# One diffusion step on one core: the turn stage joined into the hyena stage, its first folds taken tile by tile, and half of the filter's lower parts on VectorE

## The reference

```python
h = _rmsnorm(x, norm1_g) * (1.0 + scale1) + shift1
proj = h @ w_in
q, k, v, u_hy, gates = jnp.split(proj, SPLITS, axis=-1)
...
o_attn = _diff_attention(q_att, k_all, v_all, lam, lam_init, attn_subln_g)
o_hy = _hyena(u_hy, conv_w, conv_b, ...)
g_attn, g_hy = jnp.split(jax.nn.sigmoid(gates), 2, axis=-1)
merged = g_attn * (o_attn @ w_br_attn) + g_hy * (o_hy @ w_br_hy)
x = x + gate1 * (merged @ w_out)
h2 = _rmsnorm(x, norm2_g) * (1.0 + scale2) + shift2
x = x + gate2 * (jnp.square(jax.nn.relu(h2 @ w_up)) @ w_down)
```

```python
def _hyena(u, ...):
    u = _short_conv(u, conv_w, conv_b)
    v, x1, x2 = jnp.split(u, 3, axis=-1)
    hf = _hyena_filters(L, w1, b1, w2, b2, w3, freq)
    z = x1 * _fftconv(v, hf[:, 0], hy_bias[0])
    return x2 * _fftconv(z, hf[:, 1], hy_bias[1])
```

## Time and profile before

| | |
|---|---|
| median of three runs | 2918.12 us (2911.11 to 2922.55) |
| the profiled execution | 2921.78 us |
| its span | 2920.0 us |
| TensorE busy | 2699.8 us, 92% |
| VectorE / ScalarE / GpSimd busy | 43% / 31% / 28% |
| DMA over the span | 329.99 MB, mean 113 GB/s |
| granted TensorE clock, mean | 0.962 |

### The profile page before, as it was taken

How to read it: one execution, slowest core, us unless ns; L and a number is a source line. 1 busy time by engine, 2 the same in 40 slices (tenths; PEclk the granted TensorE clock), 3 DMA queues, 4 the chain that set the end, 5 groups by cost and what they waited for, 6 DMA issues and landing times. The chain is left out here.

```text
span 2920.0 us, 36034 instructions
## 1 busy us (share of the span) xinstructions
PE 2699.8 (92%) x14723; PEld 2312.2 (79%) x14723; DVE 1260.9 (43%) x1874; ACT 901.1 (31%) x1510; POOL 814.5 (28%) x567
## 2 busy tenths in 40 slices
PE   9757999989999999998888799798999999999998
PEld 7546887878888898887667588687888888888886
DVE  6466664445656445443677521226212212212215
ACT  2333221045555454553311331214121121121121
POOL 2565885111000110100233132212232232232330
PEclk9968999999999999999899799899999999999999
DMA  5756775442213321302766533510111111111101
GB/s 182 228 176 234 232 238 192 142 161 98 82 64 104 109 86 60 109 32 80 284 201 229 181 128 125 205 44 30 37 42 38 37 37 37 44 37 37 37 29 73
DMA packets 103938, 329.99 MB, mean 113 GB/s; under 512 B 12497, under 2 KB 30515, under 8 KB 103390
## 3 DMA queue, kind: packets, MB, share of 16 engines
q1 hardware_dynamic: 77038, 233.30, 23.2%
q0 software_dynamic: 26736, 94.38, 9.5%
HBM read 240.61 MB, written 78.64 MB: 109 GB/s over the span
## 5 line engine op out<-in xcount | busy, mean ns | idle before, releaser
L89 PE MATMUL tl_b<-tl_hi,tl_whi 128*128 128x512 f32 (+1 forms) x960 | 344.8, 359 | 20.8 <-DVE tl_lo L2350 15.0
L90 PE MATMUL tl_b<-tl_lo,tl_whi 128*128 128x512 f32 (+1 forms) x960 | 342.4, 357 | 0.0
L91 PE MATMUL tl_b<-tl_hi,tl_wlo 128*128 128x512 f32 (+1 forms) x960 | 341.7, 356 | 0.0
L2291 DVE SCALAR_TENSOR_TENSOR tl_x<-tl_b,all_mod,tl_x 128x512 f32<-128x512 f32 (+1 forms) x216 | 142.5, 661 | 374.6 <-PE tl_b L91 363.0
L2185 POOL TENSOR_TENSOR tl_wlo<-tl_raw,tl_whi 128x1024 fp32r<-128x1024 f32 x72 | 178.2, 2477 | 444.9 <-ACT tl_whi L2104 444.9
L89 PE MATMUL tl_b<-tl_uhi,tl_whi 128*128 128x512 f32 (+1 forms) x768 | 275.2, 358 | 3.5 <-POOL tl_ulo L2195 3.5
L91 PE MATMUL tl_b<-tl_uhi,tl_wlo 128*128 128x512 f32 (+1 forms) x768 | 276.6, 360 | 0.0
L89 PE MATMUL at_out<-h_hi,at_whi 128*128 128x424 f32 (+1 forms) x672 | 264.1, 393 | 12.4 <-POOL at_wlo L496 10.6
L90 PE MATMUL tl_b<-tl_ulo,tl_whi 128*128 128x512 f32 (+1 forms) x768 | 274.5, 357 | 0.0
L681 DVE TENSOR_REDUCE at_nmax<-at_s 128x1 f32<-128x1280 f32 (+1 forms) x160 | 196.8, 1272 | 112.1 <-PE at_s L548 111.4
L496 POOL TENSOR_TENSOR at_wlo<-at_raw,at_whi 128x1024 fp32r<-128x1024 f32 x28 | 66.2, 2363 | 626.7 <-ACT at_whi L597 626.7
(11 more groups left out here) (290 smaller groups left out, 5810.5 us busy)
## 6 DMA issues: line engine op xcount, KB each, us to landing
tl_raw<-in_w_tail SPq DMA_DIRECT2D x72, 512.0 KB, 3.5
hy_tab<-in_hy_tab POOLq DMA_DIRECT2D x68, 512.0 KB, 5.0
hd_wa<-in_w_adaT SPq DMA_DIRECT2D x32, 512.0 KB, 4.4
at_raw<-in_w_proj SPq DMA_DIRECT2D x28, 512.0 KB, 4.7
fd_in<-in_xT SPq DMA_DIRECT2D x16, 640.0 KB, 4.2
s_gatesT<-at_pad SPq DMA_DIRECT2D x16, 640.0 KB, 2.9
mg_gate<-s_gatesT SPq DMA_DIRECT2D x16, 640.0 KB, 5.2
fd_in<-in_w_ada SPq DMA_DIRECT2D x16, 512.0 KB, 3.6
```

The source lines that it names most:

```text
L89: pe.matmul(out, w_hi, x_hi, start=first, stop=False)
L90: pe.matmul(out, w_hi, x_lo, start=False, stop=False)
L91: return pe.matmul(out, w_lo, x_hi, start=False, stop=last)
L2291: dve.scalar_tensor_tensor(out=x1[:, n, at:at + m], in0=bank[x % GEMM_BANKS][:, 0:m], scalar=g.mod[:, gate, SEG_OF[c]:SEG_OF[c] + 1], in1= ...
```

## The change

It has three parts.

1. **v comes earlier.** In attention, at step 71 (the second unit of the last head), SP loads v's four row tiles from convT into the places of the q and k buffers that head 6 has left. Hyena finds them there: its `v` lies at the same addresses, within the space that the spectra's products (`gc`, `gs`) will use later.
2. **Turn is gone; hyena does its work.** TensorE transposes v at hyena's start (`turn_v`), ACT moves z and splits the folds alternately, and DVE folds as tiles come. The first two forward steps run together (TOGETHER = 2), over one time tile after the other, each waited for alone, which needs four table units at once. Forward steps rotate over four bank pairs (FWD_PAIR). The inverse of tile 0 waits for the lower parts frequency tile by frequency tile, and its runs are reordered (PARTS) so that both halves' first four frequency tiles come first and p is whole after the third run; ACT copies it then. x1 isn't stored transposed any more: SP loads its four row tiles, two of them only when DVE has read the last spectrum of order 0, over whose buffers they lie, and TensorE transposes eight blocks behind each inverse tile of order 0 (`turn_x1`); DVE multiplies with them in their bank. The first two spectra of order 1 are loaded only after the last of these. POOL's wait for all lower parts (L1618) and its order are otherwise as before.
3. **Head.** In order 1 DVE makes 11 of the 21 lower parts (ON_DVE: pair 0's five, none of pairs 1 and 2, four of pair 3, two of pair 4), with a semaphore for each pair. The last four squared tiles are no longer added by DVE: TensorE sums each over the partitions, ten columns a tile (`token_sum`), and DVE adds the five sources. The modulations come ahead of the last pairs.

```diff
+                if u == HY_V_AT:
+                    sp.wait_ge(conv_out, 16 * U_U)
+                    for m in range(2):
+                        sp.wait_ge(qk[m], (HEADS - 1) * UNITS)
+                    for c in range(CHT):
+                        sp.dma_start(hy_v[c][:], g.convT[c]).then_inc(hy_v_in, 16)
...
+    LATE_SUMS = list(range(len(SQUARE_AT), KD))
+    SOURCES = 1 + len(LATE_SUMS)
+    ON_DVE = [range(5), (), (), range(4), range(2)]
...
                     for i, x in enumerate(slots(p)):
+                        if o and i in ON_DVE[p]:
+                            continue
                         pool.wait_ge(split_hi, o * SPLITS + SLOTS[p] + i + 1)
                         pool.tensor_tensor(lo_of(x), eo[(o * PAIRS + p) % 2][:, i], hi_of(x), ALU.subtract
-                                           ).then_inc(split_lo, 1)
+                                           ).then_inc(lows[p] if o else split_lo, 1)
...
+            def token_sum(src, x):
+                for tt in range(TT):
+                    mm = pe.matmul(p_sum[:, src, tt:tt + 1], x[:, tt * P:(tt + 1) * P], g.ones[:, 0:1], start=True,
+                                   stop=True)
+                mm.then_inc(token_sums, 1)
+            def late_sum(n):
+                k = LATE_SUMS[n]
+                pe.wait_ge(squared, k + 1)
+                token_sum(n + 1, stream[(X_AT + k) % STREAM])
...
                 if o == 0:
                     for p in range(len(EARLY), PAIRS):
                         taps_of(1, p)
-                    pe.wait_ge(summed, KD)
-                    evacuated(pe, R - 1)
-                    evacuated(pe, R - 2)
-                    evacuated(pe, R - 3)
-                    for tt in range(TT):
-                        mm = pe.matmul(p_sum[:, tt:tt + 1], acc[:, tt * P:(tt + 1) * P], g.ones[:, 0:1], start=True,
-                                       stop=True)
-                    mm.then_inc(token_sums, 1)
+                        if p == len(EARLY):
+                            for x in range(R - NB, R):
+                                evacuated(pe, x)
+                            pe.wait_ge(summed, len(SQUARE_AT))
+                            token_sum(0, acc)
+                        elif p < PAIRS - 1:
+                            late_sum(0)
+                    for n in range(1, len(LATE_SUMS)):
+                        late_sum(n)
...
             def pair(o, p):
                 k = o * PAIRS + p
                 eo_k = eo[k % 2]
-                if k >= 2:
+                if 2 <= k < PAIRS + 2:
                     dve.wait_ge(split_lo, slots_before(k - 1))
+                elif k >= 2:
+                    dve.wait_ge(lows[p - 2], len(slots(p - 2)))
                 dve.wait_ge(taps, 2 * k + 2)
...
+            def lower_slots(p):
+                for i, x in enumerate(slots(p)):
+                    if i in ON_DVE[p]:
+                        dve.wait_ge(split_hi, SPLITS + SLOTS[p] + i + 1)
+                        dve.tensor_tensor(lo_of(x), eo[(PAIRS + p) % 2][:, i], hi_of(x), ALU.subtract
+                                          ).then_inc(lows[p], 1)
...
+                modulations()
+                lower_slots(0)
                 for p in range(len(EARLY), PAIRS):
                     pair(1, p)
-                    sum_up(len(SQUARE_AT) + p - len(EARLY))
-                sum_up(KD - 1)
-                dve.wait_ge(token_sums, 1)
-                dve.tensor_scalar(var[:], p_sum[:], 1.0 / D, EPS, ALU.mult, ALU.add).then_inc(var_done, 1)
+                    lower_slots(p)
+                dve.wait_ge(token_sums, SOURCES)
+                dve.tensor_reduce(tot[:], p_sum.rearrange("p s t -> p t s"), AX.X, ALU.add).then_inc(tot_done, 1)
+                dve.wait_ge(tot_done, 1)
+                dve.tensor_scalar(var[:], tot[:], 1.0 / D, EPS, ALU.mult, ALU.add).then_inc(var_done, 1)
                 dve.wait_ge(std_done, 1)
                 dve.reciprocal(rstd[:], std[:]).then_inc(rstd_done, 1)
...
-def stage_turn(nc, g, z):
...
+PARTS = [(0, 0), (1, 1), (0, 1), (1, 0)]
+FWD_PAIR = [[0, 1, 2, 3, 0, 1, 2, 3, 0, 1], [1, 3, 2, 0, 1, 3, 2, 0, 1, 0]]
+TOGETHER = 2
...
-        spec = [st.sb(f"spec{s}", [P, SPEC, CH]) for s in range(2)]
+        spec_at = st.place()
+        spec = [st.sb(f"spec{s}", [P, SPEC - s, CH]) for s in range(2)]
+        x1 = [st.over(f"x1{c}", spec_at + c * 4 * T, [P, T]) for c in range(2)] + [
+            st.sb(f"x1{c}", [P, T]) for c in range(2, CHT)]
...
         def _(sp):
+            sp.wait_ge(tab_in[2 * TOGETHER - 1], 16)
             sp.dma_start(bias[:], g.d["hy_bias"]).then_inc(bias_in, 16)
+            for c in range(2, CHT):
+                sp.dma_start(x1[c][:], g.convT[CHT + c]).then_inc(x1_in, 16)
+            sp.wait_ge(fwd_read, FTILES)
+            for c in range(2):
+                sp.dma_start(x1[c][:], g.convT[CHT + c]).then_inc(x1_in, 16)
...
+            def turn_v(n):
+                mirror, tile = JOBS[n]
+                if n >= 4:
+                    pe.wait_ge(z_moved, n - 3)
+                for c in range(CHT):
+                    mm = pe.transpose(bank[4 + n % 4][:, c * P:(c + 1) * P], v[c][:, stored_columns(mirror, tile)],
+                                      g.ident[:])
+                mm.then_inc(v_turned, 1)
+            def turn_x1(tile):
+                if tile == 0:
+                    pe.wait_ge(x1_in, 16 * CHT)
+                    pe.wait_ge(fwd_read, FTILES)
+                else:
+                    pe.wait_ge(zdone, tile)
+                for mirror in range(2):
+                    for c in range(CHT):
+                        mm = pe.transpose(bank[mirror][:, c * P:(c + 1) * P], x1[c][:, stored_columns(mirror, tile)],
+                                          g.ident[:])
+                mm.then_inc(x1_turned, 1)
+            def banks_free(o, j):
+                pairs = FWD_PAIR[o]
+                if pairs[j] in pairs[:j]:
+                    last = max(x for x in range(j) if pairs[x] == pairs[j])
+                    pe.wait_ge(fwd_read, o * FTILES + last + 1)
+                elif o == 0 and pairs[j] >= 2:
+                    pe.wait_ge(z_moved, len(JOBS))
+                elif o and pairs[j] == 0:
+                    pe.wait_ge(zdone, HT)
+                elif o and pairs[j] == 1:
+                    pe.wait_ge(fwd_read, FTILES)
+                elif o:
+                    pe.wait_ge(q_read, HT if pairs[j] == 2 else HT - 1)
+            def forward(o, j, c, tiles, last):
...
+                for tile in tiles:
+                    mm = products(pe, forward_banks(o * FTILES + j)[c][:], t_hi[:, at + tile], t_lo[:, at + tile],
+                                  hi[:, tile], lo[:, tile], tile == first, tile == last)
+                if tiles[-1] == last:
+                    mm.then_inc(runs, 1)
+            for n in range(LAT_JOBS):
+                turn_v(n)
             for o in range(2):
...
+                for j in range(TOGETHER):
+                    banks_free(o, j)
+                for tile in range(HALF_T[0]):
+                    pe.wait_ge(fold_lo, o * HT + tile + 1)
+                    for j in range(TOGETHER):
+                        for c in range(2):
+                            forward(o, j, c, [tile], HALF_T[0] - 1)
+                    if o == 0 and tile == 0:
+                        for n in range(LAT_JOBS, len(JOBS)):
+                            turn_v(n)
+                for j in range(TOGETHER, FTILES):
+                    banks_free(o, j)
+                    if j == LAT_FT:
+                        pe.wait_ge(fold_lo, o * HT + HT)
+                    tiles = range(HALF_T[0]) if j < LAT_FT else range(HALF_T[0], HT)
                     for c in range(2):
...
+                        forward(o, j, c, tiles, tiles[-1])
+                for i in range(HT):
+                    n = o * HT + i
+                    if i < 2:
+                        pair = 2 + n % 2
+                        last = max(x for x in range(FTILES) if FWD_PAIR[o][x] == pair)
+                        pe.wait_ge(fwd_read, o * FTILES + last + 1)
+                    else:
+                        pe.wait_ge(q_read, n - 1)
+                    for x, (q, half) in enumerate(PARTS):
+                        hi, lo = (gs_hi, gs_lo) if half else (gc_hi, gc_lo)
+                        odd = half ^ q
+                        if i < HALF_T[0]:
+                            unit, at = FWD_U + 4 * i + x, 0
+                            tiles = range(LAT_FT // 2 * odd, LAT_FT // 2 * (odd + 1))
...
                         for k, tile in enumerate(tiles):
+                            if i == 0 or i == HALF_T[0]:
+                                pe.wait_ge(g_lo, 2 * (o * FTILES + tile + 1))
+                            mm = products(pe, bank[4 + 2 * (n % 2) + q][:], t_hi[:, at + k], t_lo[:, at + k],
+                                          hi[:, tile], lo[:, tile], x < 2 and k == 0,
```

(25 more changed lines are left out.)

188 lines of the change are left out of this document (72 added, 116 removed).

## The result

The changed kernel takes 2893.28 us (median of 4 runs, 2890.10 to 2895.84) against 2919.92 before (median of 4, 2911.11 to 2922.55): 26.6 us less, ratio 0.9916, 95% interval 0.9900 to 0.9931. The forecast was 2894.5. The profiled executions are further apart, 2921.78 and 2890.10 (spans 2920.0 and 2888.3): 31.7 us.

A forecast was written before the change was run, and what follows sets the result against it. TensorE, busy 92% of the span, was taken as the bound, so gains come from shortening its gaps. Hyena -18.3 and head -5.3 sum to -23.6: 2898.2 us profiled, 2894.5 for the median, range 2880 to 2909.

The forecast's parts named there:

- Hyena, predicted -18.3: All of hyena: earlier start, later loads in both orders and an earlier p copy together save 18.3 us.
- Start, -27.4: Start of hyena: with v resident and no turn stage, first product at 1384.7 instead of 1412.15; bounds 24.5 to 29.
- Order 0, +7.3 +2.0 -3.2: Hyena's first order: late loads until inverse tile 1 ends +7.3 us, x1's transposes +2.0, order 1 starting sooner -3.2.
- Order 1, +3.6 -0.6: Hyena's second order: the same late tables cost 3.6 us up to inverse tile 1's end; earlier p copy saves 0.6.
- the two queue orders that the prediction named: POOL's queue in hyena: unit 5's table behind spectrum 2 (4.6 us gap), table 21 behind all lower parts (about 7).
- Rival 1: Hyena's feed is not short, queues run further ahead: 6.6 us off each order, 2881 us; chance 0.24.
- rival 3: Hyena's forward passes: starved feed leaves a gap and half clock each round, +20 us, 2938; chance 0.06.
- Head, predicted -5.3: Head: divided lower parts and sums on TensorE bring order 1's first product to 177.8 from 183.11; bounds 0 and 10.
- the chain is now splits and pairs, not sums: Head, before order 1's first product: last split ends at 170.3, TensorE's token sums already at 168.4.
- Rival 2: The head brings nothing and hyena's late loads take the longest landing, 12.7 us back, 2907; chance 0.17.
- Step 7 of order 0: Hyena's forward pass: this step ends at X+39.9, X being the end of the joined first four runs.
- The bounds of 3, 5 and 4 us: Uncertainty of hyena's start (3), the head (5) and the feed (4), given as 2885 to 2904 around 2894.5.

The follow-up runs named there:

- e3: Changed kernel, but all of v turned and four folds done before hyena's first product; hyena from last attention output to merge 249.28 us, by medians 8.2 slower than the changed kernel.
- e4: Changed kernel, but v loaded after the last head's last output instead of during that head; hyena from last attention output to merge 249.82 us, +7.1.
- e5: Changed kernel, but GpSimd's forward loop issues each table a step earlier and ahead of the spectrum; hyena 13.9 us shorter, 10.6 by the medians.
- e7: Changed kernel, but table 21 and the four tables behind it issued ahead of GpSimd's wait for the last lower parts; hyena 6.4 us shorter, 6.5 by medians.
- e1: Kernel before with only the head's part of the change; 10.7 us less than before, ratio 0.9967 (0.9953 to 0.9980).
- e8: Changed kernel, but x1's first two parts issued at the eighth and ninth product, tenth spectrum in the p copies' place; hyena 242.50 us, -0.2; medians 1.0 apart.
- e11: Changed kernel with the edits of e5, e7 and e8 together; 2861.18 us (2853.36 to 2869.10), ratio to before 0.9813.
- e2: Changed kernel with the old head, so only the turn and hyena's part; 17.9 us less than before, ratio 0.9940 (0.9925 to 0.9955).
- e6: Changed kernel, but table 21 alone issued ahead of GpSimd's wait for the last lower parts; hyena 2.9 us shorter, 3.7 by the medians.

## Why the prediction was right, step by step

**Hyena, predicted -18.3, measured 260.99 to 242.72 = -18.27.** That the sum is exact to a tenth is luck in part; the terms are off by up to 1 us, each way.
- Start, -27.4: measured -27.74. e3 and e4 give two shares of it, 6.6 for going tile by tile and 7.1 for v's early load. The rest is x1's transposes and the chain in front of them.
- Order 0, +7.3 +2.0 -3.2 = +6.1: from first product to first product of order 1 it took 112.56 before and 1488.15-1369.84 = 118.31 after, +5.75. Inside it the joined steps ended at 1382.0, 12.1 us after the first product instead of 14.8, because the first product already ran in 0.50 us; the stall for table 5 was 3.92 instead of 4.6, its slow clock 2.7 instead of 1.5; the last lower part stood 56.8 us behind the joined steps (56.6 predicted), tile 1 began 61.4 behind them (61.3), x1's wait and its transposes before it.
- Order 1, +3.6 -0.6 = +3.0: measured (1601.55-1488.15)-(1634.39-1524.71) = +3.7, with the two stalls where they were expected, 3.96 and 5.82 us.

The mechanism was right as well: e5 and e7 took the two queue orders that the prediction named out of the way, and the stalls went, 13.9 and 6.4 us. Of the signs it named, the first product stands 11.0 us after the last output (10 to 12), the table waits are 3.92 and 3.96 (4 to 5), inverse tile 1 starts 7.15 us after tile 0 in order 0 and 5.82 in order 1 (about 7), and the last transposes of x1 wait 2.31 (2 or less). Rival 1, a feed that isn't short, is refuted by the 15.3 us of table waits; rival 3 by there being one such stall in each forward pass and not six.

**Head, predicted -5.3: right in size, wrong in what ends the chain.** Nine profiles with the changed head (the changed kernel, e1, e3 to e8, e11) have a head stretch of 36.8 us in the mean, 5.1 less than 41.84. But "the chain is now splits and pairs, not sums" fell. Counted from the end of order 0 (141.3 there, 134.8 here), the prediction had the last split end at 29.0, the sums at 27.1 and the first product at 36.5. Measured: VectorE done with the last pair's lower parts at 26.2, the sums at 31.3, the first product at 37.6. Pairs and splits were 2.5 us quicker, the sums 4.2 slower, since the row that I had taken at 2.2 us a sum ran at 1.2 GHz, 4.3 each (granted clock 0.50 from 134.6 to 175.6); VectorE stood 5.09 us for it. The pairs were quicker since VectorE's five lower parts for pair 0 took 5.25 us, not the 8.7 of strict alternation: GpSimd's first part waited for ScalarE's split until 136.57, so three of the five ran alone at 0.68 us, and only the last two took 1.75 each. In the three profiles where the row of three sums took 9.8 us instead of 12.96 (part of it at the full clock) the stretch is 34.3 to 34.5, otherwise 36.5 to 38.7. Rival 2 is refuted: e1 has the head's gain without hyena's change, and the stalls are 3.9 us, not longer.

**Slips in the working.** Step 7 of order 0 comes to X+39.5 and not 39.9 (11.5 and five times 5.6), and inverse tile 1 of order 1 was given 12.8 us where order 0 had 12.3, without a reason. The bounds of 3, 5 and 4 us give 2882.5 to 2906.5 when added up, not 2885 to 2904. The tables' waits before the change are 0.8 us in all, not 1 to 2. Rival 3's limit, a gap of 2.2 us behind which products run at 1.2 GHz, isn't one: the last section has a gap of 2.31 us with either outcome.

**What the prediction left out.** The nine profiles are 1.2 us quicker from order 1's first product to the heads' first (60.5 in the mean, before and e2 61.5 and 62.0), and 1 to 2 us quicker through heads and attention (1126.6 in the mean; 1128.8 and 1127.3). With these, hyena and head add up to 18.3+5.1+1.2+1.4 = 26 us, the 26.6 of the medians. Which transfer or wait gives them wasn't tried. The merge and what follows took 1285.6 before and 1284.8 to 1287.3 in all others: no part of the difference.

**The profile against the profile** (31.7 us) is 6.5 ahead at the end of order 0, not of the change's making, then 4.2 head, 1.6, 2.3, 18.3 hyena, and -1.1 after it.

## What to carry to other kernels

When work is joined or moved so that it ends sooner, read the queue that loads its operands from front to back: a transfer behind a wait for another engine is late for everyone behind it. Move the whole run of loads, not the one that the profile names (e6 against e7), and take waits that stand one behind the other away together (e8 alone 0.2 us, in e11 part of 8.6). Compare variants by a stretch that repeats, beside the median: here the hyena stretch repeated within 1.2 us, where whole times of one kernel moved by 6 to 16. And read the clock from the spacing of matmuls where the trace has no record of it yet.
